# First mixing of a two-block layer: weight steps placed ahead of scores and transposes on TensorE, softmax, scans and closing product ahead of low parts on VectorE, two low parts on GpSimd

## The reference, cut to what matters

```python
h = jnp.concatenate([meta, x], axis=1)                  # 16 + 256 rows
z = rmsnorm(h, g_pre_mix) @ w_in
q, k, v, xr, yr = jnp.split(z, split_at, axis=-1)       # widths 512, 128, 128, 512, 512
s = einsum(q, k) * scale                                # two blocks of 128 queries, 8 heads of 64
s = where(valid, s, NEG)                                # window of 128 keys
m = maximum(max(s), sink)
p = exp(s - m); denom = sum(p) + exp(sink - m)
attn = einsum(p / denom, v)
xr = causal_depthwise_conv(xr, conv_w, conv_b)          # 4 taps
r, i = sigmoid(xr @ w_a + b_a), sigmoid(xr @ w_x + b_x) # block-diagonal gates
log_a = -8 * r * softplus(-lam)
a = exp(log_a); mult = sqrt(-expm1(2 * log_a))
h_t = a_t * h_(t-1) + mult * i * xr                     # a scan along the tokens
rec = gelu(yr) * h_t
mix = concatenate([attn, rec]) @ w_out
```

## Time and profile before

| | us |
|---|---|
| median of 3 runs (888.41 to 888.63) | 888.44 |
| profiled execution, its own time | 888.37 |
| its span in the trace | 886.6 |

### The profile page before, as it was taken

How to read it: one execution, slowest core, us unless ns; L and a number is a source line. 1 busy time by engine, 2 the same in 40 slices (tenths; PEclk the granted TensorE clock), 3 DMA queues, 4 the chain that set the end, 5 groups by cost and what they waited for, 6 DMA issues and landing times.

```text
span 886.6 us, 17878 instructions
## 1 busy us (share of the span) xinstructions
PE 874.9 (99%) x7067; PEld 811.9 (92%) x7067; DVE 585.6 (66%) x950; ACT 525.3 (59%) x927; POOL 24.6 (3%) x36
## 2 busy tenths in 40 slices
PE   9999999999999999999999999999999999999997
PEld 6988899999998999999999999999988999999986
DVE  4689865555556666668787878556767555554576
ACT  6478664444446765665968676765558444444463
POOL 4100300000000000000000000000000000000000
PEclk9999999999999999999999999999999999999999
DMA  9913775555554464545324142335565565565541
GB/s 282 271 65 112 199 199 190 188 188 188 189 189 143 143 190 143 161 151 163 125 67 144 50 143 77 116 122 170 185 201 191 190 189 189 189 189 189 183 150 48
DMA packets 107655, 143.24 MB, mean 162 GB/s; under 512 B 3032, under 2 KB 95448, under 8 KB 107600
## 3 DMA queue, kind: packets, MB, share of 16 engines
q1 hardware_dynamic: 105648, 137.60, 48.4%
q0 software_dynamic: 1744, 4.67, 2.4%
q10 hardware_dynamic: 208, 0.20, 0.1%
HBM read 141.41 MB, written 1.05 MB: 161 GB/s over the span
## 4 chain that ended last, share of the span: by engine, by line
PE 90%; DVE 5%; ACT 4%; issue 1%; DMA 0%; DVEq 0%; ACTq 0%
PE ps L1853 17%; PE ps L1855 16%; PE ps L1854 16%; PE ps L1859 9%; PE ps L1861 9%; PE ps L1860 9%; PE ps L2237 2%; PE ps L2224 1%; PE ps L2245 1%; ACT wh L640 1%; PE ps L1951 1%; PE ps L2212 1%; DVE wl L1214 1%; DVE R L1250 0%; PE ps L1932 0%
## 5 line engine op out<-in xcount | busy, mean ns | idle before, releaser
L1214 DVE TENSOR_TENSOR wl<-w_raw,wh 128x1024 fp32r<-128x1024 f32 x251 | 304.7, 1223 | 216.2 <-ACT wh L640 215.6
L1853 PE MATMUL ps<-xTh,wh 128*128 128x256 f32 (+1 forms) x1160 | 331.2, 286 | 1.3 <-DVE xTl L1240 0.8
L1855 PE MATMUL ps<-xTh,wl 128*128 128x256 f32 (+1 forms) x1160 | 326.3, 281 | 0.0
L1854 PE MATMUL ps<-xTl,wh 128*128 128x256 f32 (+1 forms) x1160 | 326.3, 281 | 0.0
L640 ACT ACTIVATE wh<-w_raw 128x1024 fp32r<-128x1024 f32 x251 | 263.6, 1055 | 80.0 <-PE ps L1861 58.9
L1853 PEld LDWEIGHTS ps<-xTh,wh 128*128 128x128 f32 x1160 | 219.0, 189 | 5.3 <-issue 3.2
L1854 PEld LDWEIGHTS ps<-xTl,wh 128*128 128x128 f32 x1160 | 218.3, 188 | 1.9 <-issue 1.0
L1855 PEld LDWEIGHTS ps<-xTh,wl 128*128 128x128 f32 x1160 | 219.3, 189 | 0.0
L1859 PE MATMUL ps<-wh,y 128*128 128x512 f32 x224 | 87.9, 392 | 0.0
L1861 PE MATMUL ps<-wh,y 128*128 128x512 f32 x224 | 87.6, 391 | 0.0
L1860 PE MATMUL ps<-wl,y 128*128 128x512 f32 x224 | 87.1, 389 | 0.0
(11 more groups left out here) (390 smaller groups left out, 1265.3 us busy)
## 6 DMA issues: line engine op xcount, KB each, us to landing
w_raw<-in_w_in_dram SPq DMA_DIRECT2D x42, 1024.0 KB, 5.2
w_raw<-in_w_ff_dram SPq DMA_DIRECT2D x32, 1024.0 KB, 5.3
w_raw<-in_w_ffn_gate_dram SPq DMA_DIRECT2D x11, 1024.0 KB, 5.4
w_raw<-in_w_ffn_up_dram SPq DMA_DIRECT2D x11, 1024.0 KB, 5.3
w_raw<-in_w_ffn_down_dram SPq DMA_DIRECT2D x11, 1024.0 KB, 5.0
w_raw<-in_w_out_dram SPq DMA_DIRECT2D x8, 1024.0 KB, 4.9
w_raw<-in_w_proj_a_dram SPq DMA_DIRECT2D x4, 1024.0 KB, 5.4
w_raw<-in_w_proj_b_dram SPq DMA_DIRECT2D x4, 1024.0 KB, 5.3
```

The source lines that it names most:

```text
L1214: TT(low_part, raw_unit(SLOT[p], j, layout), high_part.bitcast(F32), ALU.subtract).then_inc(w_lo, 1)
L1853: mm(out, wh_, xh, start=first, stop=False)
L1854: mm(out, wh_, xl, start=False, stop=False)
L1855: return mm(out, wl_, xh, start=False, stop=last)
```

## The change: order on TensorE and VectorE, and two low parts on GpSimd

On TensorE, two steps of `rec_unit(0)` move ahead of `scores(0)` and of the wait for the query copies, one step of `rec_unit(2)` moves ahead of `scores(1)`, and three steps of `gelu_unit(1)` move ahead of `p_transposes(0)`. On VectorE, `soft_sums(1)` moves ahead of `lo(13)`, `lo(14)` moves ahead of the argument of the square root, and `lo(16)` and `lo(17)` are no longer there, so that `oT_lo(1)`, the scans and the closing product follow each other; ahead of `lo(18)` there is a wait for all low parts up to 17. GpSimd does `lo(16)` and `lo(17)` with the same subtraction, each after the high part is there and the low parts before it are done.

```diff
 # GpSimd
+            for n in (16, 17):
+                pool.wait_ge(w_hi, n + 1)
+                pool.wait_ge(w_lo, n)
+                high_part, low_part = unit_parts(n, "rows")
+                pool.tensor_tensor(low_part, raw_unit(SLOT[n // 2], n % 2, "rows"), high_part.bitcast(F32), ALU.subtract).then_inc(w_lo, 1)
             pool.wait_ge(gain_used, 1)
...
 # VectorE
             lo(12)
+            soft_sums(1)
             lo(13)
-            soft_sums(1)
...
             link(TT(a2, a_, a_, ALU.mult))
+            lo(14)
             dve.wait_ge(a_tanh_out, 2 * LT)
             STT(th_, a2, 1.0, th_, ALU.add, ALU.mult).then_inc(m2_out, 1)
             oT_lo(0)
-            lo(14)
             lo(15)
             dve.wait_ge(mult_out, 1)
             link(TT(xc, a2, xc, ALU.mult))
             oT_lo(1)
-            lo(16)
             for m in range(LT):
                 ins = dve.tensor_tensor_scan(...)
             link(ins)
-            lo(17)
             dve.wait_ge(gelu_out, 1)
             TT(gy, gy, r_g[:, :, META:T1], ALU.mult).then_inc(rec_out, 1)
+            dve.wait_ge(w_lo, 18)
             lo(18)
...
 # TensorE
+            steps = rec_unit(0)
+            some(steps, 2)
             for b in range(2):
                 pe.wait_ge(emptied[b], EMPTIED[6][b])
             scores(0)
-            rec_unit(0)
-            rec_unit(1)
+            run(steps)
+            run(rec_unit(1))
+            steps = rec_unit(2)
+            some(steps, 1)
             scores(1)
-            rec_unit(2)
-            rec_unit(3)
-            gelu_unit(0)
+            run(steps)
+            run(rec_unit(3))
+            run(gelu_unit(0))
+            steps = gelu_unit(1)
+            some(steps, 3)
             p_transposes(0)
-            gelu_unit(1)
+            run(steps)
```

More of the change, by code:

```diff
@@ L2047, in rec_unit, with some @@
             def rec_unit(m):
-                run(fm_steps(6 + m, xTh, xTl, 0, T1))
+                return fm_steps(6 + m, xTh, xTl, 0, T1)
             def gelu_unit(m):
-                run(fm_steps(10 + m, xTh, xTl, META, S))
+                return fm_steps(10 + m, xTh, xTl, META, S)
+            def some(steps, n):
+                for _ in range(n):
+                    next(steps)
+            steps = rec_unit(0)
+            some(steps, 2)
             for b in range(2):
@@ L2073, in _ @@
             p_transposes(1)
[L2074 to L2077, removed]
+            run(gelu_unit(2))
+            steps = gelu_unit(3)
+            some(steps, 2)
             outputs(1)
```

## The result

| | before | after |
|---|---|---|
| median of 20 runs each, us | 888.74 (888.22 to 889.31) | 890.39 (889.84 to 891.54) |
| ratio | | 1.002, interval 1.0014 to 1.0026 |
| profiled execution, its own time | 888.37 | 890.50 |
| its span | 886.6 | 888.7 |

The changed kernel is 1.65 us slower, with an interval that leaves out no change. The forecast was 889.1 and "the same"; 890.39 lies inside the stated range of 888.6 to 890.5, but close to the port rival's 890.2 and not to the forecast.

A forecast was written before the change was run, and what follows sets the result against it. The prediction took TensorE, busy for 99% of the span, as the bound. It summed 888.37 - 0.6 (scores) + 1.4 (unit 11) - 0.08 (second transposes) = 889.1 us, with a stated range of 888.6 to 890.5.

The forecast's parts named there:

- port rival: At the scan's input: VectorE waits until GpSimd's lo(16) is through, TensorE stops for 1.1 us; 890.2 us, chance 0.35.
- The bound: Whole kernel: TensorE, busy for 99% of the span, is the bound; any new wait of it is lost in full.
- the gain at the scores: Ahead of the first scores: two moved steps cover TensorE's wait for the query copy, a gain of 0.6 us.
- Unit 11: Ahead of the first transposes: moved steps make TensorE wait 1.6 us for lo(11), a loss of 1.4 us.
- The second softmax sums: Ahead of the second transposes: the move is worth 1.13 us, the late copy eats it, about 1.0 of waiting stays.
- I take 0 by those rows: At the scan's input: GpSimd reading two SBUF operands beside VectorE was taken to cost 0.
- GpSimd's own duration: GpSimd's moved low parts: each subtraction takes 2.35 us by the nearest row, hidden from TensorE.
- the rival of a slow GpSimd: Low parts 16 and 17: at twice the row's time TensorE loses 0.7 us, 889.8; slow GpSimd or both, chance 0.08.
- VectorE's slack: At the recurrent low part: it ends well before TensorE wants it, so taking two low parts off VectorE gains 0.
- the line for "slower": On the measured time: slower counts from 890.2 us, as 0.2%, 1.8 us, tells from no change; chance of slower 0.25.

The follow-up runs named there:

- e10: Kernel before the change with only the two steps of rec_unit(0) moved ahead of the first scores; 888.07 us against 888.64.
- e4: Kernel before the change with only the three steps of gelu_unit(1) moved ahead of the first transposes; 890.87 us against 888.50.
- e5: Kernel before the change with only low parts 16 and 17 on GpSimd and VectorE's wait ahead of lo(18); 889.74 us against 888.54.
- e1: Changed kernel with low parts 16 and 17 back on VectorE at their old places; 889.11 us against 888.50.
- e6: Changed kernel with low parts 16 and 17 back on VectorE, plus one unneeded GpSimd subtraction of two SBUF operands; 890.53 us against 888.54.
- e7: Changed kernel with low parts 16 and 17 back on VectorE, plus an unneeded GpSimd zero fill that reads nothing; 889.02 us against 888.54.
- e11: Kernel before the change with only the second softmax sums moved ahead of lo(13); 888.44 us against 888.64.
- e3: Changed kernel with low parts 16 and 17 back on VectorE and gelu_unit(1) whole behind the first transposes; 887.78 us against 888.50.
- e8: e3 without the step ahead of scores(1), oT_hi(1) ahead of ScalarE's square root, oT_lo(1) and lo(16) in VectorE's wait for it; 887.09 us against 888.54.

## Why the prediction was wrong, step by step

**The bound, and the gain at the scores: right.** The scores begin at 39.20 - 38.23 = 0.97 behind the last query matmul (0.84 before) with six matmuls done; alone that edit gives -0.57 (e10), against 0.6. The step ahead of `scores(1)` filled no wait in any trace. (In the earlier trace rows's list the wait at the scores is not one of the two largest, as the prediction has it, but the fifth longest; nothing hangs on that.)

**Unit 11: right in kind, 0.2 too large.** The idle time, released by VectorE's low part, is where it was put, 1.25 us against 1.6. TensorE started unit 11 at 58.17 - 0.30 = 57.87 on the clock of before, against 58.10: VectorE had moved by 0.57 instead of 0.43 (`lo(11)` at 56.90 - 0.30 = 56.60 against 57.17), and TensorE followed the low part's end by 0.05, not by the 0.14 that I took from the transposes. So the second transposes are late by 0.51, not 0.72. e4 shows the term by itself.

**The second softmax sums: right.** The move is worth about 1.1 and was eaten by the late copy: 0.99 of idle time is left ahead of the second transposes, as forecast.

**GpSimd: the step that failed.** "I take 0 by those rows" was the wrong end. The rows that I took it from have VectorE reading one operand from PSUM, and in the changed kernel such an operation still takes 0.69 beside GpSimd. They said nothing of an operation that reads two operands from SBUF. The rival had the place, the order and the price: the scan's input held until `lo(16)` is through, a stop of TensorE ahead of the second token block, put at 1.1. It measured 1.32 in the stretch: from 81.91, a spacing of 0.23 further, to 83.28 are 1.14, and the remaining 0.18 lies in the matmuls behind, of which the first pair is 0.34 apart (as behind the wait in e5, 90.48 to 90.82); what slows the ones beyond it stays open. With e1, e6 and e7 the cause is shown: it goes when the subtraction goes, comes with one that nobody needs, and stays away with a fill. The Trainium skill, "SBUF — State Buffer", section "Who interferes with whom", states that a VectorE instruction with two SBUF inputs contends with a GpSimd instruction that reads SBUF, not with one that only writes it, and that the order of issue decides who is blocked. Here the trace agrees: 2.89 and 2.92 us in place of 1.28 beside a subtraction, 1.29 beside a fill, and in e5, where VectorE came first, 1.28 for its product and 3.30 for the subtraction. I gave this rival 0.35 on the ground that no row had such an effect. But no row could have had it: GpSimd never read SBUF beside such an operation before. The absence of a case was read as evidence. That the rival's sum, 0.72 + 1.1 = 1.82, meets the stretch's +1.83 so closely is luck: unit 11 in it is 0.2 too large and the stop 0.2 too small.

**GpSimd's own duration: right.** 2.41 us for 128 partitions (e6, and the shorter of the two in the changed kernel), against 2.35 for 16. TensorE had no wait for low part 16 or 17; the rival of a slow GpSimd falls.

**VectorE's slack: right for the change, not in general.** That nobody waited for the recurrent low part held for the forecast, where TensorE comes late. e5 and e11 show that with TensorE on time it is among the next things to be late.

**The chances.** Forecast and port differ by 1.1 us, and the line for "slower", 890.2, lay at the port's own value; a wrong choice at one term decided the verdict. That line took 0.2% as the least change that can be told; the 20 runs of each kernel give the ratio to 0.06% either way.

## What to carry to other kernels

A step that is moved ahead of a wait brings its own waits along: look up in the other engine's list where the thing that it waits for stands, and if that is behind the very operation whose wait was to be filled, the wait grows by one operation, and every consumer behind it moves (e4: one edit, 2.4 us). Work moved to an idle engine need not be free: here two low parts on GpSimd cost 1.0 to 1.3 us through VectorE. For elementwise work on GpSimd, list VectorE's two-operand SBUF instructions in the same stretch, and take rows that lack the case as a missing price, not as a price of zero. When an idle time of the bounding engine is closed, the next things that it needs must come earlier as well; e11 won 1.1 us at one wait and kept 0.15; e3 won 1.70 at the second transposes and kept 0.74, while e8, with the low parts moved into VectorE's idle time, won 1.68 there and kept 1.67.

## What the runs showed of the hardware that was not expected

A VectorE instruction that is held up by GpSimd does not show as idle time: its row grows (1.28 to 2.89 and 2.92, four scans from 2.56 to 4.03 and 6.21), so a list of waits misses it, and only the duration of the same operation in another trace gives it away. GpSimd's row grows too: in the changed kernel its second subtraction takes 3.24 beside the product and the scans, against 2.41 for the first, which came before the product. Between the four scans the two engines seem to take turns: in e5 GpSimd's two subtractions end inside the scans' 6.21 us, the second at 82.36 + 2.64 = 85.00, and from there to the scans' end at 86.81 are 1.81 us, about three of the four scans at their length of before (an estimate from 2.56 for four); the rows don't resolve the order further. A fill of 128x2400 on GpSimd, 2.12 us, costs VectorE's product nothing (1.29).
